# A float32 kernel of two small models on one core: products with few rows spread over four column groups, and a tile's transposes moved forward

## The reference

```python
def hybrid_layer(h, pos, norm_g, w_in, b_forget, lam_q1, lam_k1, lam_q2, lam_k2,
                 subln_g, w_out, lambda_init):
    bsz, length, _ = h.shape
    u = rms_norm(h, norm_g)
    proj = jnp.einsum('bld,dp->blp', u, w_in)
    split_points = np.cumsum(SPLITS)[:-1].tolist()
    dq, dk, dv, dz, fq, fk, fv, fz, f_logit = jnp.split(proj, split_points, axis=-1)
...
    log_f = jax.nn.log_sigmoid(f_logit.astype(jnp.float32) + b_forget.astype(jnp.float32))
    cum = jnp.cumsum(log_f, axis=1).transpose(0, 2, 1)
...
    mixed = jnp.concatenate([o_a * jax.nn.silu(dz), o_b * jax.nn.silu(fz)], axis=-1)
    return h + jnp.einsum('blm,md->bld', mixed, w_out)
```

## Time and profile before

| what | us |
|---|---|
| median of 3 runs | 1747.82 |
| lowest and highest run | 1747.42, 1750.42 |
| the profiled execution: span from its first to its last instruction | 1744.7 |
| TensorE busy in it | 1688.5 |
| VectorE, ScalarE, GpSimd busy | 1037.8, 395.1, 260.4 |

### The profile page before, as it was taken

How to read it: one execution, slowest core, us unless ns; L and a number is a source line. 1 busy time by engine, 2 the same in 40 slices (tenths; PEclk the granted TensorE clock), 3 DMA queues, 4 the chain that set the end, 5 groups by cost and what they waited for, 6 DMA issues and landing times.

```text
span 1744.7 us, 26319 instructions
## 1 busy us (share of the span) xinstructions
PE 1688.5 (97%) x10790; PEld 1323.8 (76%) x10790; DVE 1037.8 (59%) x2001; ACT 395.1 (23%) x1029; POOL 260.4 (15%) x339
## 2 busy tenths in 40 slices
PE   8999999999999999999998999999999999999998
PEld 7997487775799848997476878699946677477774
DVE  5777435743477747777388847387664555425463
ACT  2010023532200102010048223200102233122331
POOL 3324000000023201221003130022201210012100
PEclk9999999999999999999999989999999999999999
DMA  8666643222355445554533310254556963459730
GB/s 267 217 203 205 167 126 122 73 73 97 122 169 184 178 144 172 168 170 174 178 106 113 124 38 2 97 180 159 179 159 111 184 101 98 92 69 183 102 108 24
DMA packets 196967, 237.27 MB, mean 136 GB/s; under 512 B 28300, under 2 KB 177216, under 8 KB 196592
## 3 DMA queue, kind: packets, MB, share of 16 engines
q1 hardware_dynamic: 191872, 224.97, 45.6%
q0 software_dynamic: 4960, 10.61, 2.1%
q10 hardware_dynamic: 16, 0.00, 0.0%
HBM read 232.30 MB, written 1.07 MB: 134 GB/s over the span
## 4 chain that ended last, share of the span: by engine, by line
PE 87%; DVE 7%; ACT 3%; DMA 2%; issue 1%; POOL 0%; DVEq 0%; SPq 0%; POOLq 0%; ACTq 0%
PE ps L589 29%; PE ps L277 23%; PE ps L655 14%; PE ps L518 6%; PE ps L599 3%; PE ps L1875 2%; DMA arena<-arena 1%; PE ps L2482 1%; PE ps L2494 1%; PE ps L335 1%; PE ps L2513 1%; PE ps L1892 1%; PE ps L1702 1%; PE ps L2508 0%; PE ps L1199 0%
## 5 line engine op out<-in xcount | busy, mean ns | idle before, releaser
L277 PE MATMUL ps<-hT,ring 128*128 128x272 f32 (+4 forms) x1696 | 360.4, 368 | 4.3 <-ACT hT L359 4.0
L277 PEld LDWEIGHTS ps<-hT,ring 128*128 128x128 f32 (+1 forms) x1696 | 288.7, 191 | 58.2 <-issue 7.2
L589 PE MATMUL ps<-arena,ring 128*128 128x128 f32 x1280 | 162.5, 275 | 0.0
L655 PE MATMUL ps<-ring,arena 128*128 128x512 f32 x352 | 155.9, 593 | 1.7 <-DVE more L760 1.7
L850 POOL TENSOR_TENSOR arena<-arena 128x128 f32<-128x128 f32 x44 | 36.7, 834 | 789.9 <-DVE arena L774 446.2
L589 PEld LDWEIGHTS ps<-arena,ring 128*128 128x128 f32 x1280 | 152.6, 192 | 0.0
L589 PE MATMUL ps<-hT,ring 128*128 128x128 f32 x1280 | 150.1, 275 | 0.0
L589 PEld LDWEIGHTS ps<-hT,ring 128*128 128x128 f32 x1280 | 146.5, 192 | 0.0
L655 PEld LDWEIGHTS ps<-ring,arena 128*128 128x128 f32 x352 | 66.6, 190 | 87.2 <-issue 87.2
L589 PE MATMUL ps<-arena 128*128 128x128 f32 x960 | 120.3, 275 | 0.0
L589 PEld LDWEIGHTS ps<-arena 128*128 128x128 f32 x960 | 113.6, 192 | 0.0
(11 more groups left out here) (482 smaller groups left out, 2691.4 us busy)
## 6 DMA issues: line engine op xcount, KB each, us to landing
ring<-in_ffn_w_gate SPq DMA_DIRECT2D x44, 1024.0 KB, 5.2
ring<-in_ffn_w_up SPq DMA_DIRECT2D x44, 1024.0 KB, 7.1
ring<-in_ffn_w_down SPq DMA_DIRECT2D x44, 1024.0 KB, 4.9
ring<-in_w_in SPq DMA_DIRECT2D x32, 1024.0 KB, 12.5
ring<-in_ab_w_in SPq DMA_DIRECT2D x12, 1024.0 KB, 5.2
ring<-in_w_out SPq DMA_DIRECT2D x8, 1024.0 KB, 4.9
ring<-in_ab_w_out SPq DMA_DIRECT2D x6, 1024.0 KB, 4.8
ring<-in_c_w_k SPq DMA_DIRECT2D x4, 1024.0 KB, 6.5
```

What stands on the lines that cost most here:

```text
L277: last = nc.tensor.matmul(o, l, r, start=(i == 0), stop=(i == len(pairs) - 1))
L589: m = nc.tensor.matmul(o, left[:, k, :], right[:, k, :], start=(k == 0), stop=(k == 3))
L655: return nc.tensor.matmul(ps[:, BANK[i], :], hid[p][:, left, :], right, start=(p == 0), stop=(p == LAST))
```

## The change

There are four edits. (1) The leading tokens' output product leaves the common k loop. `meta_rows` makes it between tile 0's end and tile 1's, with each k's 1024 output columns in four pieces of 256, piece g written to partitions 32g to 32g + 15 of bank 4. The stationary is the same for the four; the partitions choose the column group of the array. It counts `y_done` second instead of first, and the first weight slot of the product is released in it (k = 2) instead of after k = 1 of the common loop. (2) ScalarE and VectorE treat the leading tokens behind tile 0's norm; VectorE's add is in four pieces. (3) The forget gate's product is divided in the same way by tokens, four pieces of `LQ` = 68, and VectorE's bias addition too. (4) `trans_pe(pe, 1)` comes behind the third half product in layer 0 and behind the second in layer 1, instead of behind the fourth.

```diff
--- before.py
+++ after.py
@@ -465,9 +465,10 @@
                 act.wait_ge(y_bias_in, act_b())
                 nc.scalar.activation(x_ss[:, 1:2], y_ss[:, 1:2], ACT.Sqrt, scale=1.0 / D, bias=y_bias[:, 0:1]).then_inc(x_rooted, 1)
                 return
-            meta_norm_act(act, True)
             for t in range(T):
                 x_norm_act(act, t)
+                if t == 0:
+                    meta_norm_act(act, True)
                 h_out_act(act, t, col)
 
         def hybrid_end_dve(dve, col):
@@ -475,13 +476,16 @@
             if col is None:
                 hybrid_final_dve(dve)
                 return
-            dve.wait_ge(y_done, dve_y())
-            nc.vector.tensor_tensor(xm[:, :], xm[:, :], ps[0:META, 4:6, :].rearrange("p a b -> p (a b)"), ALU.add).then_inc(m_new, 1)
             for t in range(T):
                 dve.wait_ge(y_done, dve_y())
                 nc.vector.tensor_tensor(x[:, t, :], x[:, t, :], ps[:, 2 * t:2 * t + 2, :].rearrange("p a b -> p (a b)"), ALU.add).then_inc(x_new, 1)
                 x_norm_dve(dve, t)
                 if t == 0:
+                    dve.wait_ge(y_done, dve_y())
+                    for g in range(4):
+                        c = slice(256 * g, 256 * (g + 1))
+                        m = nc.vector.tensor_tensor(xm[:, c], ps[32 * g:32 * g + META, 4, 0:256], xm[:, c], ALU.add)
+                    m.then_inc(m_new, 1)
                     meta_norm_dve(dve)
                 h_out_dve(dve, t, col)
                 if t == 0:
@@ -513,13 +517,23 @@
 
             def rows(t, k, halves=(0, 1)):
                 n = s0 + k // 2
-                o = ps[:, 2 * t:2 * t + 2, :] if t < T else ps[0:META, 4:6, :]
+                o = ps[:, 2 * t:2 * t + 2, :]
                 for h in halves:
                     m = nc.tensor.matmul(o[:, h, :], lhs(k, t), slot2(n)[:, k % 2, h * 512:(h + 1) * 512],
                                          start=(k == 0), stop=(k == nk - 1))
                 return m
 
-            tiles = ([T] if meta else []) + list(range(T))
+            def meta_rows():
+                for k in range(nk):
+                    for g in range(4):
+                        m = nc.tensor.matmul(ps[32 * g:32 * g + META, 4, 0:256], lhs(k, T),
+                                             slot2(s0 + k // 2)[:, k % 2, 256 * g:256 * (g + 1)],
+                                             start=(k == 0), stop=(k == nk - 1), skip_group_check=True)
+                        if k == 2 and g == 0:
+                            m.then_inc(slot_used, 1)
+                m.then_inc(y_done, 1)
+
+            tiles = list(range(T))
             for k in range(ahead):
                 if k % 2 == 0:
                     take_slot(pe, s0 + k // 2)
@@ -531,9 +545,11 @@
                 ready(k)
                 for t in tiles[:-1] if k < ahead else tiles:
                     m = rows(t, k)
-                if k % 2 == 1:
+                if k % 2 == 1 and not (meta and k == 1):
                     m.then_inc(slot_used, 1)
             for t in tiles:
+                if meta and t == 1:
+                    meta_rows()
                 if final and t == T - 1:
                     for h in range(2):
                         for k in range(nk - lag, nk):
@@ -2335,6 +2351,7 @@
         fmh = arena[:, 0:16 * L2].rearrange("p (i n) -> p i n", i=16)
         hmT = arena[:, 4352:4352 + KD * L2].rearrange("p (k n) -> p k n", k=KD)
         KB, PW = 96, 288
+        LQ = L2 // 4
         vraw = arena[:, 6528:6528 + 4 * PW].rearrange("p (b n) -> p b n", b=4)
         tokv = arena[0:KB, 7680:7680 + 3 * D].rearrange("p (b n) -> p b n", b=3)
         zraw = arena[:, 10752:10752 + KD * L2].rearrange("p (k n) -> p k n", k=KD)
@@ -2436,7 +2453,8 @@
                 raw_n[FT[p]] = n = f_turn()
                 fc = slice(f_cols(layer, FT[p][0]).start, META + P)
                 group(f_bank(layer, n)[:, fc], [(slot8(s + p % 2)[:, k, (p // 2) * P:(p // 2 + 1) * P], hT[:, k, fc]) for k in range(KD)])
-            trans_pe(pe, 1)
+                if p == 2 - layer:
+                    trans_pe(pe, 1)
             need_h(pe, pe_h.n)
             for p in range(4):
                 fc = slice(META + P, L2)
@@ -2457,7 +2475,13 @@
                 if p == 7:
                     take_slot(pe, s)
                     x_turn()
-                    group(ps[0:8, 7, 0:L2], [(slot8(s, 8)[:, k, :], hT[:, k, :]) for k in range(KD)], frees=True).then_inc(x_ready, 1)
+                    for k in range(KD):
+                        for g in range(4):
+                            m = nc.tensor.matmul(ps[32 * g:32 * g + 8, 7, 0:LQ], slot8(s, 8)[:, k, :], hT[:, k, LQ * g:LQ * (g + 1)],
+                                                 start=(k == 0), stop=(k == KD - 1), skip_group_check=True)
+                            if k == 0 and g == 0:
+                                m.then_inc(slot_used, 1)
+                    m.then_inc(x_ready, 1)
                     s += 1
                 kind, i = FT[p - 1] if p > 0 else ("", 0)
                 if kind in ("dv", "fv"):
@@ -2598,7 +2622,10 @@
                     dlink(dve, nc.vector.tensor_tensor(nlam, nlam, lam[:, 1:2], ALU.subtract))
                 if p == 7:
                     dve.wait_ge(x_ready, dve_x())
-                    nc.vector.tensor_scalar(fl, ps[0:8, 7, 0:L2], forget[:, layer:layer + 1], None, ALU.add).then_inc(x_taken, 1)
+                    for g in range(4):
+                        m = nc.vector.tensor_scalar(fl[:, LQ * g:LQ * (g + 1)], ps[32 * g:32 * g + 8, 7, 0:LQ], forget[:, layer:layer + 1],
+                                                    None, ALU.add)
+                    m.then_inc(x_taken, 1)
                 if p == 9:
                     dve.wait_ge(fl_log, layer + 1)
                     dlink(dve, nc.vector.scalar_tensor_tensor(fl2, fl, 0.0, fl2, ALU.min, ALU.subtract))
```

## The result

Over 20 runs of each kernel, the median was 1746.19 us before and 1733.18 us after the change; the ratio is **0.9926, interval 0.9905 to 0.9947**. That is 13.0 us less, where the forecast had 13.7 less and 1734.1 us. The profiled execution after the change has a span of 1729.4 us, 15.3 less than that before.

What follows compares the result with a forecast made beforehand. TensorE, busy 97% of the span, was taken as the bound. Product −10.9, transposes −1.3 and −1.5, gate 0 sum to −13.7 us; on the three-run median of 1747.82 that gives 1734.1 us, range 1728.5 to 1740.5.

Steps and rivals of the forecast that it cites:

- The 3.1 us added to the span: Whole kernel: the three-run median, 1747.82 us, lay this far above the profiled span, so the forecast was raised by it.
- The product: Layer 0's output product: the leading tokens' part falls from 14.8 to 3.9 us in four column groups, −10.9 us.
- The step from two column groups (L1735) to four: Leading tokens' product: four groups assumed to run together in the 3.60 us that L1735 takes with two.
- Rival B: Leading tokens' product: only two column groups run together, −10.1 us in all, 1737.7 us; chance 0.11.
- C: Split products: the column groups follow one another, −3.6 us in all, 1744.2 us; chance 0.06.
- a cover of 3.5: Behind tile 0: leading rows ready 8.1 us after the sum, their transposes due at 11.6, so no wait.
- Rival E: Layer 1's start: the postponed 1 MB weight load delays its first copies, 3 to 5 us back, 1737 to 1739; chance 0.05.
- The transposes: Second half's transposes, both layers: issued sooner, they remove TensorE's waits, −1.3 us in layer 0 and −1.5 in layer 1.
- The gate: Forget gate, both layers: TensorE's list 2.55 us shorter each, but taken back by later waits; 0, bounds −5.1 and +1.8.
- this price: Layer 0 behind longer idling: the granted clock may fall to the 1.2 GHz level, costing 1.8 us.
- Waits of 3 to 5 us near 1385 and 1590: Before the scores of both layers: TensorE idle this long, as a sign that the forecast is right.
- The copies' chain: Rotation copies, two buffers in turn: a shorter gate does not bring them forward, so TensorE waits for rotated tiles.

Runs made afterwards that it cites:

- e6: The changed kernel with two column groups in place of four, for the leading tokens' product and the gate; 1735.82 us, ratio 0.9945 to the kernel before.
- e7: The changed kernel with the same pieces all in one column group (sums wrong, read for time only); 1742.67 us, ratio 0.9979 to the kernel before.
- e2: The kernel before with only the leading tokens' product split and moved, gate and transposes as before; 1732.69 us, ratio 0.9933.
- e4: The changed kernel with the forget gate alone put back as it was; 1729.28 us, ratio 0.9899 to the kernel before.
- e1: The kernel before with only the second half's transposes moved; 1740.69 us, ratio 0.9968.
- e3: The kernel before with only the forget gate split into four column groups; 1746.19 us, ratio 1.0010.
- e5: The changed kernel measured once more, unaltered; 1733.42 us, ratio 0.9928 to the kernel before.
- e8: The changed kernel with four buffers for the rotation copies in place of two; 1721.06 us, ratio 0.9861 to the kernel before.
- e10: The changed kernel with four rotation buffers and the old gate; median 1733.38 us, called of no use, its three lowest runs 1725.25 to 1725.85.
- e11: The changed kernel with four rotation buffers, measured again; 1720.33 us, ratio 0.9834 to the kernel before.
- e12: The changed kernel with four rotation buffers and VectorE's rotation ahead of its wait for the exponential; 1718.63 us, ratio 0.9825 to the kernel before.

## Why the prediction was right, and where it was not

**The number.** That the forecast of 1734.1 us came within 1 us of 1733.18 is in part luck. The three executions behind 1747.82 lie 1.6 us above the median of 20, 1746.19; from that one the same sum gives 1732.5 us. The 3.1 us added to the span aren't a launch's share either: in every run on record span and time differ by 1.8 to 1.9 us, and the profiled execution was simply some 1.3 us below the median. The saving of 13.0 us has an interval of about 3.7 us to either side, so it confirms the sum of 13.7 and not its small terms.

**The product.** Forecast −10.9 us, measured −10.97 in every profile with four groups. The step from two column groups (L1735) to four held: 3.65 us for an estimate of 3.6 to 3.9. Rival B would have been 7.05, as e6 shows, and C 13.99, as e7 shows. The Trainium skill (TensorE: Matmul & The Clock Gate, Part 3) gives 2.38× for three column tiles, which made an estimate of 4.3 us; the runs decide for 3.65, a factor of 3.83 from one group to four. The same part says that a weight load overlaps running products only when its row group differs, and in another place allows it into a background weight buffer too; e7 has one row group and one column group, and its loads are hidden, so the first of the two doesn't hold here as it stands.

**What lies around the product.** VectorE's add took 1.70 us for 1.7 (tile 0's chain of 3.75 us is 3.72 by its own rows), the leading rows ready 3.6 us early for a cover of 3.5, the delayed load without a waiter. Rival E (3 to 5 us back in layer 1) finds no support: layer 1 takes 159.0 and 158.2 us in e2 and e4, which have the moved slot, and 157.0 in e1, which hasn't, a difference of 1 to 2 us between single profiles.

**The transposes.** Forecast −2.8 us. The two waits are gone in all kernels that have the edit; e1 alone gave 3.35 us, with an interval that reaches from 0.0 to some 11 us. The size is thus shown by the vanished idle time and fits the times, but these don't fix it.

**The gate.** TensorE's list lost 2.6 us a layer (3.76 to 1.13), as forecast. That it keeps none of it held on the whole: e3's ratio is 1.0010, and e4, without the gate, has a lower ratio than the change, within the intervals. Where it went, single profiles show in part. Layer 0 takes 168.5 and 168.9 us (the change, e5) against e4's 171.4, so there some 2.7 us were kept, though e3 against before kept nothing. Layer 1 takes 162.5 and 163.4 against 158.2. Between the change and e4 in layer 1 this is the gate's −2.6, +3.3 for what ran at low clock (16 records of 256 columns 6.46 us at 1591.79 for 3.72 at full clock, the four ahead of them 1.33 for 0.80), and +3.3 of waiting (1.56 + 1.83 + 1.76 against e4's 0.59 + 1.31), 4.0 of the 4.4 us. The 1.76 and the 1.31 are waits beside GpSimd's addition, which the prediction didn't see.

Two profiles don't size the clock's term, since the profile before has 6.8 us of low clock in layer 1 as well. The mean granted clock of each execution is on record and says more. Its median is 0.988 to 0.989 in the kernel before (chips of e1 to e7), e1, e2 and e4, and 0.986 to 0.987 in e3, the change and e5, the kernels with the gate in four groups and two buffers. 0.002 of 1745 us are an estimated 3.5 us, of the 5.3 that the two gates gave. The forecast had this price once, 1.8 us, in layer 0, and expected less than half of it. There it was 1.65 us (5.58 in place of 3.93). So the clock's term was put too low; the 0 came out because the list's gain of 5.3 us covers about what clock and waits take.

**Where it would wait.** Waits of 3 to 5 us near 1385 and 1590 were forecast. What came were several of 1.6 to 1.9 us, the first at 1371, right behind the gate, where VectorE's own order sets the end. Waits as long as forecast came near both places in other kernels of the set: 3.94 us at 1590.4 in e5, 4.69 at 1390.9 and 3.44 at 1595.6 in e6. "The copies' chain" as the holder was right for layer 1 (e8, e10), save for the wait beside GpSimd's addition, and wrong for the first wait of layer 0 (e11, e12). The earlier trace rows showed two later waits of layer 0 and left out the one at 1372.99, 1.32 us, which was the next to grow.

## What to carry to other kernels

A product whose stationary side is narrow can be split by its moving columns over TensorE's column groups; here the gain was the number of groups, almost in full. Before shortening TensorE's list, look for the next wait behind the edit and ask what issues what it waits for: a copy that waits for a buffer keeps its time whatever TensorE does, and two more buffers were worth as much as the whole change. An idle stretch of an engine in front of work that is already possible is a matter of order.

## What the runs showed of the hardware

Waits of TensorE of 1.83 and 1.88 us were followed by a granted clock of 0.50, for 6.8 and 3.4 us in the change. At 1371 the wait is 0.56 us longer than before, and the low clock behind it costs 1.65 us more: the price is several times the idle time that was added. The length of a wait alone doesn't decide. 1.32 us at the same place was followed by low clock in e1 and e4 (from 1374.4 and 1375.0 on) and not in the kernel before, and waits of 2.04 us (e7, 1393.16) and 2.17 us (e1, 1392.11) were followed by none. The four longest waits, 3.44 to 4.69 us (e3, e5, e6), all have it beside or behind them. With no wait over 0.7 us left in the layers (e12), no stretch of them ran at low clock.

In the profiles, instructions of VectorE that combine two tiles of SBUF are drawn out while GpSimd adds 2176 columns (4.78 us): 0.42 us became 4.02 us at 1601.46, with the end 0.3 us behind GpSimd's. A copy out of PSUM beside it kept its 0.28 us. TensorE waited up to 2.78 us behind such an instruction. This is read from the profiles; no run takes the addition away.
